# Seven products instead of eight for 5 of 22 K-tile pairs of a decoder trunk's down projections

## What is computed

```python
def swiglu(x, w_up, w_down):
    g, u = jnp.split(x @ w_up, 2, axis=-1)
    return (jax.nn.silu(g) * u) @ w_down
...
h = h + 0.5 * rms_norm(swiglu(rms_norm(h, ffn1_pre[l]), ffn1_up[l], ffn1_down[l]), ffn1_post[l])
h = h + rms_norm(mix, mix_post[l])
h = h + 0.5 * rms_norm(swiglu(rms_norm(h, ffn2_pre[l]), ffn2_up[l], ffn2_down[l]), ffn2_post[l])
```

## Time and profile before

| | us |
|---|---|
| median of 3 timed runs | 2388.61 |
| lowest and highest of them | 2387.86 and 2389.59 |
| the profiled execution, its span (first to last instruction) | 2387.2 |
| PE busy in it | 2370.4 (99%) |
| DVE busy in it | 1644.4 (69%) |
| ACT busy in it | 1207.4 (51%) |
| POOL busy in it | 200.2 (8%) |

### The profile page before, as it was taken

The page is one execution under the profiler, slowest core; times in us unless marked ns, Lnnn a source line. Parts: engine busy times, 40 slices in busy tenths (PEclk is TensorE's granted clock), DMA queues, the critical chain, the costliest instruction groups (busy, mean ns, idle before and its releaser), DMA issues.

```text
span 2387.2 us, 34469 instructions
## 1 busy us (share of the span) xinstructions
PE 2370.4 (99%) x10667; PEld 1955.8 (82%) x10667; DVE 1644.4 (69%) x1905; ACT 1207.4 (51%) x1444; POOL 200.2 (8%) x392
## 2 busy tenths in 40 slices
PE   9999999999999999999999999999999999999998
PEld 7888888888887888888888888888788888888887
DVE  5999999974456655655545545555799999996444
ACT  5555555554445454454544444444655555555443
POOL 1212112110000000000000000000021212111000
PEclk9999999999999999999999999999999999999999
DMA  7666666666656565565666666655566666666664
GB/s 234 219 212 207 219 208 226 209 221 184 204 173 192 158 185 172 161 189 158 200 188 197 190 195 192 194 182 186 176 210 222 215 214 205 218 211 225 192 194 155
DMA packets 265731, 470.99 MB, mean 197 GB/s; under 512 B 21056, under 2 KB 54512, under 8 KB 265296
## 3 DMA queue, kind: packets, MB, share of 16 engines
q1 hardware_dynamic: 252752, 453.04, 60.6%
q0 software_dynamic: 12752, 17.24, 2.3%
q10 hardware_dynamic: 176, 0.07, 0.0%
HBM read 456.64 MB, written 2.10 MB: 192 GB/s over the span
## 4 chain that ended last, share of the span: by engine, by line
PE 96%; DVE 2%; issue 1%; DMA 1%; ACT 0%; DVEq 0%; POOL 0%; ACTq 0%; SPq 0%; POOLq 0%
PE acc L684 24%; PE acc L686 24%; PE acc L685 24%; PE acc L775 5%; PE acc L776 5%; PE acc L777 5%; PE bank L775 2%; PE bank L776 2%; PE bank L777 2%; PE bank L705 1%; DVE w_lo L1437 1%; DVE h L1501 0%; DVE xT_lo L1448 0%; PE bank L1011 0%; PE bank L945 0%
## 5 line engine op out<-in xcount | busy, mean ns | idle before, releaser
L1437 DVE TENSOR_TENSOR w_lo<-w_raw,w_hi 128x1024 fp32r<-128x1024 f32 (+1 forms) x856 | 1011.1, 1184 | 633.0 <-ACT w_hi L1112 628.8
L1112 ACT ACTIVATE w_hi<-w_raw 128x1024 fp32r<-128x1024 f32 (+1 forms) x856 | 880.4, 1031 | 1055.1 <-PE acc L686 810.6
L684 PE MATMUL acc<-w_hi,xT_hi 128*128 128x512 f32 x1584 | 622.5, 393 | 3.6 <-DVE xT_lo L1448 2.4
L686 PE MATMUL acc<-w_hi,xT_lo 128*128 128x512 f32 x1584 | 616.9, 389 | 0.0
L685 PE MATMUL acc<-w_lo,xT_hi 128*128 128x512 f32 x1584 | 616.7, 389 | 0.0
L684 PEld LDWEIGHTS acc<-w_hi,xT_hi 128*128 128x128 f32 x1584 | 297.4, 188 | 67.6 <-DVE xT_lo L1448 3.3
L686 PEld LDWEIGHTS acc<-w_hi,xT_lo 128*128 128x128 f32 x1584 | 297.3, 188 | 62.6
L685 PEld LDWEIGHTS acc<-w_lo,xT_hi 128*128 128x128 f32 x1584 | 297.5, 188 | 60.0
L684 PE MATMUL acc<-w_hi,act_hi 128*128 128x512 f32 x704 | 274.3, 390 | 1.5 <-DVE act_lo L1470 1.5
L686 PE MATMUL acc<-w_hi,act_lo 128*128 128x512 f32 x704 | 273.9, 389 | 0.0
L685 PE MATMUL acc<-w_lo,act_hi 128*128 128x512 f32 x704 | 273.9, 389 | 0.0
(11 more groups left out here) (206 smaller groups left out, 2128.9 us busy)
## 6 DMA issues: line engine op xcount, KB each, us to landing
w_raw<-in_ffn_up_dram SPq DMA_DIRECT2D x352, 512.0 KB, 4.2
w_raw<-in_ffn_down_dram SPq DMA_DIRECT2D x176, 512.0 KB, 4.7
w_raw<-in_w_gate_dram SPq DMA_DIRECT2D x96, 512.0 KB, 4.1
w_raw<-in_w_in_dram SPq DMA_DIRECT2D x72, 512.0 KB, 3.7
w_raw<-in_w_in_dram SPq DMA_DIRECT2D x128, 256.0 KB, 3.0
w_raw<-in_w_ret_out_dram SPq DMA_DIRECT2D x32, 512.0 KB, 4.8
w_raw<-in_w_out_dram SPq DMA_DIRECT2D x32, 512.0 KB, 4.8
act_raw<-blocks POOLq DMA_DIRECT2D x352, 32.0 KB, 3.8
```

What stands on the lines that cost most here:

```text
L684: pe.matmul(pair[m][:, :], xh, wh, start=(first and kk == 0), stop=False)
L686: mm = pe.matmul(pair[m][:, :], xl, wh, start=False, stop=(last and kk == KG - 1))
L1112: act.activation(w_hi[:, s, cols], w_raw[:, s, cols], ACT.Copy).then_inc(w_rounded, 1)
L1437: dve.tensor_tensor(w_lo[:, s, cols], w_raw[:, s, cols], w_hi[:, s, cols].bitcast(f32), ALU.subtract).then_inc(w_split, 1)
```

## The change

In each turn of a down stage, five pairs of K tiles (8 to 12) are multiplied by seven products instead of eight. The 2x2 blocks are now two token tiles by two K tiles, and two K tiles by the two output strips of the turn; so both strips are summed side by side, and the order of groups is no longer 22 and 22 but mixed (`DOWN_A`, `DOWN_B` for plain groups, `DQUADS` for those of the seven products: groups 9 and 10, 14 and 15, 20 and 21, 25 and 26, 30 and 31). Besides:

- DVE makes four sums of weight blocks for each such pair (`down_sum13`, `down_sum24` into `dt_raw`), ACT rounds them and DVE splits them in two halves (`dt_hi`, `dt_lo`). The second of the two groups is rounded and split only by half. There is one buffer of sums, where the up stages have two.
- DVE makes sums of the hidden activations in turn 0 (`hidden_sums` for the pieces p = 4, 5 and 6, into `ds_raw`), ACT rounds them (`sums_hi`) and DVE splits them (`hidden_sums_lo`).
- The sums of weights lie where `h` was. So `h` is written to `out` behind the mixer (the first time the input `x` still holds it) and loaded again after the last seven-product block of each down stage, all by DMAs on POOL's queue (`h_again`); `updates` waits for it.
- The seven products leave partial sums in four banks. ACT copies the first (`d_p1`) and DVE combines them (`d_u2` to `d_u5`). The result of a strip is now accumulator plus or minus such a sum, made by DVE into `y_ffn`; ACT squares that (`down_square`), and a further DVE instruction multiplies by the gain (`times_gain`).

```diff
+DQUADS = ((9, 10, 8), (14, 15, 9), (20, 21, 10), (25, 26, 11), (30, 31, 12))
+NDQ = len(DQUADS)
+DOWN_A = dict([(n, n) for n in range(8)] + [(22, 13), (23, 14), (24, 15), (27, 16), (28, 17), (32, 18), (33, 19), (34, 20), (35, 21)])
+DOWN_B = dict([(8, 0), (11, 1), (12, 2), (13, 3), (16, 4), (17, 5), (18, 6), (19, 7), (29, 13)] + [(36 + j, 14 + j) for j in range(8)])
+A_LAST = 35
+D_STRIPS = {4: (0, 2), 5: (2, 2), 6: (4, 1)}
...
+        h_at, ds_at = x_at - 4 * MT * D, x_at + 2 * KD * SEQ
+        dt_raw = sb("dt_raw", [P, 4, STRIP], f32, at=h_at)
+        dt_lo = sb("dt_lo", [P, 4, STRIP], f32r, at=h_at)
+        dt_hi = sb("dt_hi", [P, 4, STRIP], f32r, at=h_at + 16 * STRIP)
+        ds_raw = sb("ds_raw", [P, 4, NDQ, P], f32, at=ds_at)
+        ds_lo = sb("ds_lo", [P, 4, NDQ, P], f32r, at=ds_at)
+        ds_hi = sb("ds_hi", [P, 4, NDQ, P], f32r, at=ds_at + 16 * NDQ * P)
...
+            half = (sec in ("up0", "up1") and n in QUAD_UP) or (sec in ("down0", "down1") and n in DQ_B)
+            return slice(STRIP, KG * STRIP) if half else slice(0, KG * STRIP)
...
+                        for quads in (DQ_A, DQ_B):
+                            if n - SLOTS in quads:
+                                sp.wait_ge(t_summed, 3 * (down_quad(f, i, quads[n - SLOTS]) + 1))
+                                sp.sem_inc(slot_summed, 1)
+                        k, strip = source[n]
...
+            def h_again(f, src):
+                pool.wait_ge(t_used, down_quad(f, CH // 2 - 1, NDQ - 1) + 3)
+                for m in range(MT):
+                    pool.dma_start(h[:, m, :], src[m * P:(m + 1) * P, :]).then_inc(h_back[m], 16)
...
+            for m in range(MT):
+                wait_h(pool, 1, m, CH - 1)
+                pool.dma_start(out[0][m * P:(m + 1) * P, :], h[:, m, :]).then_inc(h_parked, 16)
...
+                pe.wait_ge(hid_split, turns(f, k // 2))
+                pe.wait_ge(w_split, group(sec, i, ng) + 1 + SLOTS)
+                p1 = three(bank[0][:, :], *x(0, 0), *w(ng, 0), first, last)
+                if last:
+                    p1.then_inc(filled[0], 1)
+                three(acc_a[0][:, :], *x(1, 0), *w(ng, 1), False, False).then_inc(w_used, 1)
+                pe.wait_ge(w_split, group(sec, i, nu) + 1 + SLOTS)
+                pe.wait_ge(ds_split, len(D_STRIPS) * f + sorted(D_STRIPS).index(k // 2) + 1)
+                three(acc_b[0][:, :], *s(3), *w(nu, 1), False, False).then_inc(w_used, 1)
+                pe.wait_ge(t_split, 2 * down_quad(f, i, j) + 1)
+                p7 = three(bank[3][:, :], *s(2), *tt(1), first, last)
+                p5 = three(bank[1][:, :], *s(0), *tt(0), first, last)
+                pe.wait_ge(t_split, 2 * down_quad(f, i, j) + 2)
+                p6 = three(bank[2][:, :], *s(1), *tt(2), first, last)
+                if last:
+                    p7.then_inc(filled[3], 1)
+                    p5.then_inc(filled[1], 1)
+                    p6.then_inc(filled[2], 1)
+                three(acc_a[1][:, :], *x(1, 1), *tt(3), False, False).then_inc(t_used, 1)
...
+                        if n in DQ_B:
+                            down_products(f, i, DQ_B[n])
+                        elif n not in DQ_A:
+                            product(n)
...
+            def down_square(f, i, k, m):
+                act.wait_ge(squares, SQUARES[f"down{f}"] + i * 2 * MT + k * MT + m + 1)
+                act.activation(four(d_p1[:, :]), y_of(y_ffn, 2 * i + k, m), ACT.Square,
+                               accum_out=sq_strip[:, k, m:m + 1]).then_inc(squares, 1)
...
+                        j, pair = DT_AT[n]
+                        both = slice(2 * pair, 2 * pair + 2)
+                        act.wait_ge(t_summed, 3 * down_quad(f, i, j) + 2 * pair + 1)
+                        act.activation(dt_hi[:, both, :], dt_raw[:, both, :], ACT.Copy).then_inc(t_rounded, 1)
+                    if n % 2 == 0 and n // 2 + 2 < NUP:
+                        with act.If(i < 1):
+                            hidden_hi(f, n // 2 + 2)
+                            if n // 2 + 2 in D_STRIPS:
+                                sums_hi(f, n // 2 + 2)
+                    if n == DQUADS[-1][0]:
...
+            def down_sum13(f, i, j):
+                sec, (ng, nu, k) = f"down{f}", DQUADS[j]
+                b = w_raw[:, ng % SLOTS:ng % SLOTS + 2, :].rearrange("p s (kk n) -> p (s kk) n", kk=KG)
+                dve.wait_ge(t_used, down_quad(f, i, j) + 2)
+                if f == 1:
+                    dve.wait_ge(h_parked, 16 * MT)
+                dve.wait_ge(w_landed[ng % SLOTS], group_landed(sec, i, ng))
+                dve.wait_ge(w_landed[nu % SLOTS], group_landed(sec, i, nu))
+                dve.tensor_tensor(dt_raw[:, 0:2, :], b[:, 0::3, :], b[:, 2:3, :].broadcast_to([P, 2, STRIP]),
+                                  ALU.add).then_inc(t_summed, 1)
+            def down_sum24(f, i, j):
+                ng = DQUADS[j][0]
+                b = w_raw[:, ng % SLOTS:ng % SLOTS + 2, :].rearrange("p s (kk n) -> p (s kk) n", kk=KG)
+                dve.wait_ge(t_summed, 3 * down_quad(f, i, j) + 1)
+                dve.tensor_tensor(dt_raw[:, 2, :], dt_raw[:, 0, :], b[:, 3, :], ALU.add).then_inc(t_summed, 1)
+                dve.wait_ge(t_summed, 3 * down_quad(f, i, j) + 2)
+                dve.tensor_tensor(dt_raw[:, 3, :], dt_raw[:, 2, :], b[:, 1, :], ALU.add).then_inc(t_summed, 1)
...
+                link(dve.tensor_tensor(s(0), a(1, 0), a(1, 1), ALU.subtract))
+                link(dve.tensor_tensor(s(1), s(0), a(0, 0), ALU.subtract))
+                dve.tensor_tensor(s(2), a(0, 0), a(1, 0), ALU.subtract)
+                dve.tensor_tensor(s(3), a(0, 1), s(1), ALU.add).then_inc(ds_summed, 1)
...
+                    if n + SLOTS in DQ_A:
+                        down_sum13(f, i, DQ_A[n + SLOTS])
+                    rest_group(sec, i, n)
+                    if n + SLOTS in DQ_A:
+                        down_sum24(f, i, DQ_A[n + SLOTS])
+                    if n in DT_AT:
+                        j, pair = DT_AT[n]
+                        both = slice(2 * pair, 2 * pair + 2)
+                        dve.wait_ge(t_rounded, 2 * down_quad(f, i, j) + pair + 1)
+                        dve.wait_ge(t_summed, 3 * down_quad(f, i, j) + 2 + pair)
+                        dve.tensor_tensor(dt_lo[:, both, :], dt_raw[:, both, :], dt_hi[:, both, :].bitcast(f32),
+                                          ALU.subtract).then_inc(t_split, 1)
+                    if n < 2 * NUP - 4:
+                        p = n // 2 + 2
+                        with dve.If(i < 1):
+                            if n % 2 == 0:
+                                if p in D_STRIPS:
+                                    hidden_sums(f, p)
+                                hidden_lo(f, p)
+                            elif p in D_STRIPS:
+                                hidden_sums_lo(f, p)
...
+                dve.wait_ge(tile0_done, AHEAD[sec] + i + 1)
+                dve.wait_ge(u4_ready, down_turn(f, i) + 1)
+                dve.tensor_tensor(y_of(y, 2 * i + 1, 0), four(acc_b[0][:, :]), four(d_u4[:, :]),
+                                  ALU.subtract).then_inc(b_combined, 1)
+                if name is not None:
+                    rest_group(sec, i, 2 * GF - 4)
+                dve.wait_ge(b_combined, down_turn(f, i) + 1)
+                add_squares(blk, sec, i, 1, 0)
+                with dve.If(i > final - 1):
+                    output_mean(blk, 0)
+                times_gain(i, 1, 0).then_inc(y_ready, 1)
...
+                wait_strip(dve, sec, i, 2 * GF - 1)
+                wait_read(dve, f"d{f}", 1, i)
+                dve.tensor_tensor(y_of(y, 2 * i + 1, 1), four(acc_b[1][:, :]), four(d_u5[:, :]),
+                                  ALU.subtract).then_inc(acc_read[pair_of(sec, 1)], 1)
+                wait_strip_read(dve, sec, i, 1)
+                add_squares(blk, sec, i, 1, 1)
```

More of the change, by code:

```diff
@@ L104, in strassen @@
             use(f"p{f}", 0, 1, 2, 3)
+        for _ in range(CH // 2):
+            use(f"d{f}", 0, 1, 2, 3)
     transposed("x0")
@@ L451, in hybrid_trunk @@
         T_AT = {ng - 3 + pair: (j, pair) for j, (ng, nu, k) in enumerate(QUADS) for pair in range(2)}
+        DT_AT = {ng - 3 + pair: (j, pair) for j, (ng, nu, k) in enumerate(DQUADS) for pair in range(2)}
         def wait_quad_used(eng, f, i, j):
@@ L1194, in output_strips @@
                     round_group(sec, i, n)
-                    if hook is not None:
-                        hook(n)
                 def tile0():
@@ L1204, in strip_done, with sums_hi @@
                     output_square(sec, i, 1, 1)
-                if name is not None:
-                    tail(sec, i, 2 * ng, CH // 2 - 1, tile0, strip_done, name, gain)
+                tail(sec, i, 2 * ng, CH // 2 - 1, tile0, strip_done, name, gain)
+            def sums_hi(f, p):
+                j, pairs = D_STRIPS[p]
+                act.wait_ge(ds_summed, len(D_STRIPS) * f + sorted(D_STRIPS).index(p) + 1)
```

(2 more changed lines are left out.)

177 lines of the change are left out of this document (145 added, 32 removed).

## The result

The changed kernel takes 2397.32 us (median of 5 runs, 2396.8 to 2398.28), against 2388.61 before: a ratio of 1.0036, 95% interval 1.0024 to 1.0049, so 8.7 us slower. The forecast was 2392.8, inside a range of 2385.0 to 2399.5; the direction was right, the size was about half of what came.

The account below looks back on a forecast made before the run. PE was taken to bound the kernel: -13.6 (matmuls) +15.0 (waits for DVE) +2.0 (first stage end) +0.75 (kernel end) = +4.15 us on 2387.2; with the median 1.4 above the profiled span, 2392.8 us, range 2385 to 2399.5.

Parts of the forecast that it names:

- What is removed: In the two down stages, 60 matmuls go at 0.2265 us each: -13.6 us.
- What DVE gets, the first wait: Block 1 of each down stage: PE waits for DVE's second split of weight sums, 4.8 us with the start.
- check of the average: Turn 0 of a down stage: DVE gets 21 us more on 68 of 109, so on average there is room.
- Rival 1: Down stages: DVE keeps its lead as in the up stages, only the two ends cost; 2377.8 us, chance 0.07.
- rival 2: Down stages: only the first block is late, block 2 finds its sums; 2387.4 us, chance 0.18.
- The second wait: Block 2 of each down stage: PE waits again for the second split, 2.7 us with the start.
- rival 3: Block 1 of the down stages: PE's clock falls in the first wait, +2.75 us per stage; 2398.3 us, chance 0.15.
- h leaves and comes back: Behind the mixer and at down stage ends: transfers of h are hidden, zero, bounds 1 us parking, 2 per stage.
- Rival 4: Each down stage's end: the 2 MB loads hold the weights up, +2 us each; 2396.8 us, chance 0.08.
- The end of the first down stage: Making y ahead of ACT's square delays tile 1's updates, PE waits: +2.0 us.
- 3 if tile 0 is late too: End of the first down stage: upper bound of 3 us, should tile 0 be late as well.
- The end of the kernel: After the last matmul: one DVE instruction and its start go ahead of ACT's square, +0.75 us (0.7 to 0.8).

Follow-up runs that it names:

- ninth experiment: Changed kernel with activation sums spread out, both edits of the stage ends, and the five seven-product blocks moved back by one to three groups: 2379.29 us.
- experiment 1: Changed kernel with pieces 5 to 10 of the hidden activations made at steps 9, 14, 17, 20, 23, 26 of turn 0: 2386.42 us.
- experiment 2: Changed kernel with only ACT's rounding of the activation sums moved behind the next group's rounding: 2394.89 us.
- experiment 3: Changed kernel with 16 extra matmuls, their result overwritten, keeping PE busy between the halves of block 1 in turn 0: 2397.51 us.
- experiment 5: Kernel before the change with only the parking and reload of h added in both down stages: 2389.08 us.
- experiment 4: Changed kernel with group 40 split behind tile 0's updates again and the gain's product made from the accumulator's buffer while ACT squares: 2394.6 us.
- experiment 7: Changed kernel with only the gain's product moved, made from the accumulator's buffer while ACT squares: 2395.4 us.
- experiment 6: Changed kernel with only group 40's split moved back behind tile 0's updates: 2397.52 us.
- experiments 4 and 7 to 10: Includes 8, changed kernel with spread sums and both end edits: 2382.9 us; and 10, the fastest version with group 40 split ahead of updates: 2380.28 us.

## Why the prediction was right, and where it was off

**What is removed: right.** 60 matmuls at the distance of starts. The ninth experiment, where nothing waits, gives 6.65 + 6.54 = 13.2 us for the forecast's 13.6.

**What DVE gets, the first wait: right, shown.** Forecast 4.8 us with the start; the trace has 4.5 and 4.2. The forecast's check of the average, 21 us more on 68 of 109, left out the sums of activations: in turn 0 of the ninth experiment DVE is busy 30.5 us longer than before (98.4 against 67.9). The step-by-step walk had them in. The cause is the order of the queue: spreading the same work (experiment 1) takes the long wait away, and taking away the one wait for ACT (experiment 2) shortens it by 1.0. Rival 1, that DVE keeps its lead, and rival 2, that only the first block is late, were wrong for this order; the spread order with the blocks moved back is rival 1 come true, at 2379.3 for its 2377.8.

**The second wait: right in size, wrong in what took its place.** 2.7 us were forecast per stage. The first stage shows none at block 2 and 0.4 at block 3, the second 1.3, because matmuls at the low clock had let DVE catch up: 2.9 and 1.5 us. With PE kept at full clock (experiment 3) block 2 takes its 2.6, and the time is the same. So rival 3 happened, the clock fell in the first wait, but its cost was absorbed nearly whole. Without the `h` wait the first stage is 1.4 us longer than before and the second 0.3, where +0.7 each was forecast: 1.7 in all for a forecast of 1.4. That the total came so near is in part luck, since block 2's wait was traded for slow matmuls, and a block 3 that the forecast put at nothing costs 0.4 in the first stage, 0.9 at full clock. The Trainium skill ("TensorE: Matmul & The Clock Gate", section "Why this matters for your kernels") warns of idle gaps between bursts of matmuls, and here the trace agrees that the engine goes back to its lower clock (0.50 behind 4.38 us of idling); that the engine waited for has work of its own to catch up, which sets the price to nearly nothing, only the rows of experiment 3 show.

**h leaves and comes back: right, shown.** Zero (experiment 5: +0.15 us, interval -1.9 to +2.4). Rival 4 fails. 1 MB landed in 7.7 to 8.4 us there, near the 8.1 of the gains that the forecast went by; in the changed kernel it takes 9.8 and 10.1, and at the first end DVE's updates of `h` wait for nothing but POOL's power (0.47 us).

**The end of the first down stage: the term of the sum that was mis-sized.** Forecast +2.0; measured 2.3 + 2.35 = 4.65. The second of these is kv waiting for tile 1, as forecast: its updates start 5.5 us later than before, of which PE's own lateness at the stage's end is 3.3, so 2.1 later against PE. The first is tile 0, which the forecast held to be hidden. The step that failed is "the square is in at 709.5 instead of 708.86, one split of weights moves ahead of it": DVE could not start that split before 711.46, since ACT had the group's rounding behind its own square, and the sum of squares came at 712.60, 3.7 us later than before, where PE's last matmul on tile 0 was only 0.8 late (it released DVE at 708.83, and ACT at 708.03 before). POOL's power then took 0.43 longer, tile 0's updates ran 4.2 late instead of the forecast's 0.9, and the transposes waited 2.14 us. "3 if tile 0 is late too" was the bound, and below what came. Undone together, the two edits bring 1.9 us here (experiment 4). By itself neither does: with the product moved alone the split still holds the sum of squares (experiment 7), and with the split moved alone the wait goes to kv's head, where the clock falls in the trace (experiment 6). What stays in the fastest version, 2.9 us at kv's head, was not taken apart.

**The end of the kernel: mis-sized.** Forecast +0.75; measured 1.8. Two pieces were left out. POOL's power again, 0.85 us instead of 0.54. And DVE was still at tile 0's updates when PE ended, since POOL's power for that tile had also been slow (0.99). The chain that ended last in the changed kernel, in order of time, against the earlier trace rows:

```profile
2384.43 2.07 DVE h L1655 x3
2386.50 0.61 DVE y_ffn L1905
...
2388.14 0.17 DVE sq_post L1629
...
2388.64 0.86 POOL rs_post L687
```

PE's last matmul starts at 2385.31; the combination could start only at 2386.42, behind the updates. Before, ACT squared the accumulator itself at that moment, and DVE's own work was in that chain only from the sum of squares on. The forecast's words "one DVE instruction and its start go in front" priced the instruction and not the queue ahead of it. For the instruction alone the price was right: in every version with the product moved (experiments 4 and 7 to 10) this stretch is 0.8 us longer than before. The two ends are 3.7 us of the 4.5 that the forecast missed. Of the rest, 0.9 is that the median stands 2.3 above the profiled span here, not 1.4; 0.3 more in the stages and 0.4 less ahead of them nearly cancel.

## What to carry to other kernels

A busy share says whether work fits; the queue says when. 30 us of new DVE work in 109 us of a stage can leave PE without any idle time at 90% busy; at the steps where the change put pieces 5 to 10 of the activations and their sums, the same work cost 10.9 us more than with them spread. So walk the waited-for engine's queue ahead of the first use, and spread what is not yet needed until the lead is never used up.

A new instruction on an engine at the end of a stage is priced by where that engine's queue stands, not by its own 0.7 us; and where two engines stand in series, look at what each does just ahead of the handover.

An idle gap that lets the clock fall costs what nobody's catching up hides: nearly nothing at block 1, 1.3 us at kv's head in experiment 6. Fill the gap once with empty work: if the time stays, the late engine is what to mend.

## What the runs showed that was not expected

POOL's power of 128x1 took 1.00, 0.99 and 0.85 us at three of its six places in the changed kernel. It took 0.54 to 0.58 us at the other three, and 0.54 to 0.58 in every kernel where DVE's product of `y_ffn` and the gain does not run beside it. Both operands of that product lie in SBUF; before the change one of them was the accumulator in PSUM, and the power beside it took 0.57. The Trainium skill ("SBUF — State Buffer", section "SBUF: two separate sides") says that a VectorE operation with two inputs in SBUF, if it starts first, holds a pair of ports for its whole length against a GpSimd operation that reads SBUF. The trace agrees: the product runs from 712.90 to 713.59, the power from 713.03 to 714.03, 0.43 us more than alone. At the kernel's end the power starts 0.12 and 0.23 us behind the product, and ends 0.43 and 0.40 us behind the product's end, as it does here (0.44). So it looks like a wait for the product's end and not like a slower run. That the ports are the cause was not shown by itself; experiment 7 moved the product and so shows only that its place is.

The clock does not fall behind every wait of a length. In the changed kernel PE waits 0.58, 1.79 and 0.74 us at kv's head and stays at 2.4 GHz; with the order of group 40 changed it waits 1.72, 1.83 and 0.61 there, and the clock falls. Nor does the length of the wait at block 1 set for how long the clock stays low: 13 slow matmuls followed a wait of 4.38 us and 6 a wait of 4.01 in the changed kernel, but 13 a wait of 4.11 in the fourth experiment and 6 a wait of 4.36 in the sixth. What sets this the runs don't tell.
